# Two projection blocks in turn over each group of x, and first loads issued one behind another

## The chip, the cores and the metric

One core of one Trainium2 chip runs the whole program. The metric is the device time of one execution in microseconds (us), as the median of several runs. One further execution is recorded by the hardware profiler, and all rows below come from it.

## The reference, cut to what matters

The reference is a chain of transformer-like layers over 256 rows of x with 2048 columns, all in float32. Only its very first step matters here:

```
def layer_even(x, norm_g, w_in, w_out):
    h = rmsnorm(x, norm_g)                      # x * rsqrt(mean(x^2) + eps) * g
    qa, ka, ... , gate = split_cols(h @ w_in, SPLIT0)
```

`x` is 256x2048 (2 MB), `w_in` is 2048x6992. The product `h @ w_in` needs x turned (columns on the partitions) and every row scaled by its root mean square. The kernel multiplies the turned x by the gain first, forms the product, and scales the rows when the result leaves PSUM, so that the product can start before the sum of squares is known.

## The kernel before, in words

**Units and blocks.** All weights are read once, in units of 4 x 128 rows by 512 columns (1 MB). Four units (all 2048 rows) make one block of 512 result columns. Unit u of the whole program lands in slot u modulo 4 of `raw`. `plan` (L88) lays blocks one after another; `in_turn` (L98) can interleave the units of several blocks. The first ten blocks, L0_QKV, are w_in0's first columns. A block's result stands in a pair of PSUM banks, and the pairs alternate from block to block.

**Each product in three.** A float32 product is made of three cheaper ones: every weight is split in `w_hi` (ScalarE, `split_hi`, L1379) and `w_lo` = raw - w_hi (VectorE, `split_lo`, L2022), every x in `x_hi` and `x_lo`. TensorE adds w_hi x_hi, w_lo x_hi and w_hi x_lo (L685, L686, L688 or L694). One unit is 4 chunks x 2 row tiles x 3 = 24 matmuls.

**Preparing x.** x goes in four groups of 512 columns (`res`). For a group TensorE turns eight 128x128 tiles into PSUM banks 6 and 7 (`turn_group`, L784, matmuls of L781). VectorE multiplies by the gain (`gained`, L2133, two instructions). ScalarE makes `x_hi` of each (L1562), VectorE `x_lo` (L2140). The first matmul of a unit that uses a new group waits for both tiles of x_hi (`st_hi`, in `staged`, L790); the part with x_lo comes last in such a unit, behind a wait for `st_done`.

**The order.** Before, unit g of block 0 needs x group g, so four units in a row each need a new half MB of x. `first_block` turns group 1 behind the first chunk of unit 0, and group g+1 ahead of unit g after that. Units 0 and 1 are split in quarters (`first_hi`, L1385, and `first_lo`, L2028), so that a product can start when a quarter is ready. All engines run their instructions in the written order. ScalarE and VectorE split unit u+2 while unit u is multiplied (`advance`, L1494 and L2082; PARTS = 2).

**The loads.** SyncE issues all loads of x and weights. `load_block` (L508) issues x's first tile (L514), its second (L515), unit 0 in four quarters (L520), and then in turn x group 1 (L517), unit 1 (L503), group 2, unit 2, group 3, unit 3, with no wait between them. From unit 4 on a load waits until TensorE has used the unit that was in its slot (`parts_used`, L502). ScalarE issues the identity matrix and the gain columns (L1365, L1366) at the start.

**Leaving PSUM.** When a block is complete, ScalarE copies its two banks out, scaled by `rstd` (`drain`, L1403, L1416). rstd needs the squares of all four groups of x (`res_norm`, L1531, L1458). The block after next, which takes the same banks, waits for that copy.

The diff touches the plan of the first blocks (L119), the loads (L508 to L540, L575), and `first_block` on TensorE (L795, called at L1049), ScalarE (L1568, called at L1760) and VectorE (L2143, called at L2520).

Of the kernel before, what the change touches and what calls it, by code (L numbers as in the profile page):

```python
# [14 lines left out]
P = 128  # L15
SEQ = 256
NT = SEQ // P
D = 2048
KC = D // P
BW = 512  # L20
UC = 4
UNIT = UC * BW
RAW = 4
# [59 lines left out]
def build(nc, t):  # L83
# [4 lines left out]
    def plan(w, c0, widths, chunks=KC):  # L88
        first = len(blocks)
        for width in widths:  # L90
            in_turn([(w, c0, width, [(k, min(UC, chunks - k)) for k in range(0, chunks, UC)])])
            c0 += width
        return first
# [22 lines left out]
        plan(w, 2 * BW, [BW] * 2)  # L116
        return first

    L0_QKV = plan(t["w_in0"], 0, [BW] * 9 + [G0 - 9 * BW])  # L119
    L0_GATE = plan(t["w_in0"], G0, [BW] * 4)  # L120
    L0_OUT = out_blocks(t["w_out0"])
    L1_QKV = plan(t["w_in1"], 0, [BW] * 6)
# [54 lines left out]
    with ExitStack() as ctx:  # L177
# [251 lines left out]
        def first_part_landed(k):  # L429
            return first_parts_landed[k] if k < UC - 1 else raw_landed[0]  # L430
# [67 lines left out]
        def _(sp):  # L498
            def load(u, j, dst, src, first=False):

                if not first:
                    sp.wait_ge(parts_used, u - (RAW - 1))  # L502
                sp.dma_start(dst, src).then_inc(raw_landed[j], 16)  # L503

            def slot(j, chunks, width):
                return raw[:, j, :].rearrange("p (k n) -> p k n", k=UC)[:, 0:chunks, 0:width]

            def load_block(b):  # L508
                u, w, c0, width, units = blocks[b]
                for g, (k0, n) in enumerate(units):  # L510
                    if b == L0_QKV:
                        c = slice(g * BW, (g + 1) * BW)
                        if g == 0:
                            sp.dma_start(res[:, 0, c], t["x"][:, 0, c]).then_inc(x_first_tile_landed, 16)  # L514
                            sp.dma_start(res[:, 1, c], t["x"][:, 1, c]).then_inc(x_landed[0], 16)  # L515
                        else:
                            sp.dma_start(res[:, :, c], t["x"][:, :, c]).then_inc(x_landed[g], 16)  # L517
                        if g == 0:
                            for k in range(UC):
                                sp.dma_start(slot(0, UC, width)[:, k], w[k * P:(k + 1) * P, c0:c0 + width]).then_inc(  # L520
                                    first_part_landed(k), 16)
                            continue
                    j = (u + g) % RAW
                    load(u + g, j, slot(j, n, width),
                         w[k0 * P:(k0 + n) * P, c0:c0 + width].rearrange("(k p) n -> p k n", p=P), u < RAW)

            def load_units(u0, u1):
                for u in range(u0, u1):
                    b, place = block_of[u]
                    _, w, c0, width, units = blocks[b]  # L530
                    j = u % RAW
                    if b in CMP:
                        w1 = t[("cmp_k_w1", "cmp_v_w1")[CMP.index(b)]]
                        load(u, j, raw[:, j, :].rearrange("p (l n) -> p l n", l=8),
                             w1[place * 1024:(place + 1) * 1024, :].rearrange("(l p) n -> p l n", p=P))
                    else:
                        k0, n = units[place]
                        load(u, j, slot(j, n, width),
                             w[k0 * P:(k0 + n) * P, c0:c0 + width].rearrange("(k p) n -> p k n", p=P))

            def load_run(b, count):
                u, w, c0, width, units = blocks[b]

                def body(n, i, r):
                    for j, (k0, m) in enumerate(units):
                        load(n * 4 + (u + j), j, slot(j, m, width),
                             w[k0 * P:(k0 + m) * P, bass.ds(n * BW + c0, BW)].rearrange("(k p) n -> p k n", p=P))

                each(sp, count, body)
# [22 lines left out]
            def load_gain(row):  # L572
                sp.dma_start(grow, t["rows"][row:row + 1, :].to_broadcast([P, D])).then_inc(grow_landed, 16)

            load_block(L0_QKV)  # L575
            load_run(L0_QKV + 1, 8)
            load_block(L0_QKV + 9)
            for b in range(4):
                load_block(L0_GATE + b)
# [87 lines left out]
        def _(pe):  # L667
            at = [0]
# [115 lines left out]
            def turn_group(name, g, src, ready):  # L784

                for tt in range(NT):
                    ready(2 * g + tt)
                    turn(name, 2 * g + tt, [src(tt, g * UC + c) for c in range(UC)], gain=True)

            def staged(name, g, next_unit):  # L790

                pe.wait_ge(st_hi, turned_before[name] + 2 * g + 2)
                next_unit(g, lambda: pe.wait_ge(st_done, turned_before[name] + 2 * g + 2))

            def first_block(name, src, ready, next_unit):  # L795

                turn_group(name, 0, src, ready)
                if name == "n0":
                    products_of_ones(4)
                staged(name, 0, lambda g, low: next_unit(g, low, lambda: turn_group(name, 1, src, ready)))  # L800
                for g in range(1, 4):
                    if g < 3:
                        turn_group(name, g + 1, src, ready)
                    staged(name, g, next_unit)

            def tiled_first_block(name, src, ready, next_unit, others=()):

# [233 lines left out]
            def products_of_ones(n):  # L1041

                for _ in range(n):
                    nc.tensor.matmul(ps[:, 5, 0:P], ones[:], ones[:], start=True, stop=True)
# [1 line left out]
            pe.wait_ge(made["const_made"], 1)  # L1046
            products_of_ones(10)
            pe.wait_ge(ident_landed, 16)
            first_block("n0", of_res, lambda s: pe.wait_ge(x_landed[s // 2] if s else x_first_tile_landed, 16),  # L1049
                        next_in_plan)  # L1050
            advance(20)
            advance(3)

            def turn_idx(p):
# [309 lines left out]
        def _(act):  # L1364
# [34 lines left out]
            def split_next(u):  # L1399
                if u < N_UNITS:  # L1400
                    split_hi(u, u % RAW)
# [163 lines left out]
                        nc.scalar.activation(dst, ps[:, 6 + s % 2, :].rearrange("p (k n) -> p k n", k=UC),  # L1565
                                             ACT.Copy).then_inc(st_hi, 1)

            def first_block(name, gain=True, norm=None, held=False):  # L1568
                if held:
                    split_next(at[0] + 1)  # L1570
                if name == "n0":
                    first_hi(0, 1)
                hi_group(name, 0, gain)
                if name == "n0":
                    first_hi(1, UC)
                    first_hi(0, 2, 1)
                for g in range(4):
                    if g < 3:
                        hi_group(name, g + 1, gain)
                    if name == "n0" and g == 0:  # L1580
                        first_hi(2, UC, 1)
                    if norm:
                        norm(g)
                    advance(1)

            def tiled_first_block(name, norm, others=()):
# [170 lines left out]
                    act.wait_ge(x_first_tile_landed, 16)  # L1757
                act.wait_ge(x_landed[g], 16)

            first_block("n0", norm=res_norm(x_there))  # L1760
            advance(20)
            advance(3)

            def copy_idx(p):
# [244 lines left out]
        def _(dve):  # L2009
# [68 lines left out]
            def split_next(u):  # L2078
                if u < N_UNITS:
                    split_lo(u, u % RAW)  # L2080
# [59 lines left out]
                    V.tensor_tensor(x_lo[c], gained[:, tt] if gain else banks[tt], x_hi[c].bitcast(F32),  # L2140
                                    ALU.subtract).then_inc(st_done, 1)

            def first_block(name, gain=True, norm=None, held=False, update=None):  # L2143

                def ahead(g):
                    return (lambda: update(g)) if update and g < 4 else None

                if update:
                    update(0)
                lo_group(name, 0, gain, (lambda: first_lo(0, UC)) if name == "n0" else ahead(1))  # L2150
                if held:
                    split_next(at[0] + 1)
                def parts_of(g):

                    return (lambda: first_lo(0, UC, 1)) if g == 1 else (lambda: split_next(g))

                for g in range(4):
                    if g < 3:
                        lo_group(name, g + 1, gain, parts_of(g + 1) if name == "n0" else ahead(g + 2))
                    elif norm:  # L2160
                        norm()
                    advance(1, held=name == "n0" and g < 2)

            def gain_tile(name, g, tt):

# [351 lines left out]


            dve.wait_ge(cols_landed, 16)
            first_block("n0", norm=reciprocal_root)  # L2520
            advance(20)
            dve.wait_ge(const_landed, ALL_CONST)
            dve.wait_ge(made["const_made"], 1)
            all_drained(dve, L0_QKV + 6)
# [462 lines left out]
```

## Time and profile before

| what | value |
|---|---|
| median of 3 runs | 2884.12 us (2883.91 to 2885.12) |
| span of the profiled execution | 2882.2 us |
| profiled execution's own time | its span; what lies around it is not recorded (the median is 1.9 us above the span) |
| TensorE busy | 2865.5 us, 99% |
| weight loads into TensorE | 2396.2 us, 83% |
| VectorE busy | 1725.7 us, 60% |
| ScalarE busy | 1298.2 us, 45% |
| bytes moved | 530.60 MB, mean 184 GB/s |

Busy time is the time in which at least one instruction of the engine is under way. The span runs from the first to the last instruction. In timelines a bracket behind a row gives the idle time of that engine just before it and what ended it.

### The profile page before, as it was taken

What the parts mean: (1) busy time and instruction counts of PE and PEld (TensorE: products, weight loads), DVE (VectorE), ACT (ScalarE), POOL (GpSimd) and SP (SyncE); (2) the same over time, 40 slices, a digit from 0 to 9 for tenths busy, and PEclk for the clock granted to TensorE, in tenths of its full rate; (3) what the DMA queues carried; (4) which work ended last, traced back from release to release, by engine and by line L of the source; (5) the groups of instructions that cost most, each with busy time, mean ns of one, the idle gap of its engine ahead of it and who ended that gap; (6) DMA issues with size and microseconds to landing.
All of it is one profiled execution on the core that took longest, in us unless ns stands there. A gap on an engine that the chain in (4) does not pass through costs nothing.

```text
span 2882.2 us, 33404 instructions
## 1 busy us (share of the span) xinstructions
PE 2865.5 (99%) x13584; PEld 2396.2 (83%) x13584; DVE 1725.7 (60%) x1643; ACT 1298.2 (45%) x1350; POOL 14.4 (1%) x20
## 2 busy tenths in 40 slices
PE   9999999999999999999999999999999999999998
PEld 8878888888898888888888888888888888888887
DVE  5469856455565655555555677676755555555575
ACT  5344545354544533333333455545533334333354
POOL 0000000000000000000000000000000000000000
PEclk9999999999999999999999999999999999999999
DMA  7545355555445655555555557543655555555554
GB/s 249 191 157 189 116 191 179 197 178 167 156 151 198 197 191 192 192 190 193 191 190 189 190 173 245 174 150 120 224 190 189 190 190 188 190 190 192 192 180 155
DMA packets 275999, 530.60 MB, mean 184 GB/s; under 512 B 8768, under 2 KB 32464, under 8 KB 275392
## 3 DMA queue, kind: packets, MB, share of 16 engines
q1 hardware_dynamic: 274864, 527.01, 55.7%
q0 software_dynamic: 752, 2.04, 0.2%
q8 instruction: 70, 1.15, 0.2%
q10 hardware_dynamic: 288, 0.20, 0.0%
q14 instruction: 25, 0.20, 0.0%
HBM read 527.12 MB, written 2.10 MB: 184 GB/s over the span
## 4 chain that ended last, share of the span: by engine, by line
PE 96%; DVE 2%; ACT 1%; issue 1%; DMA 0%; SPq 0%; DVEq 0%; ACTq 0%
PE ps L685 29%; PE ps L686 29%; PE ps L688 27%; PE ps L694 2%; PE ps L882 1%; PE ps L781 1%; PE ps L713 1%; PE ps L714 1%; PE ps L718 1%; DVE w_lo L2025 1%; ACT w_hi L1383 1%; PE ps L869 1%; PE ps L902 1%; PE ps L913 0%; PE ps L914 0%
## 5 line engine op out<-in xcount | busy, mean ns | idle before, releaser
L2025 DVE TENSOR_TENSOR w_lo<-raw,w_hi 128x2048 fp32r<-128x2048 f32 (+3 forms) x505 | 1125.1, 2231 | 731.5 <-ACT w_hi L1383 730.6
L1383 ACT ACTIVATE w_hi<-raw 128x2048 fp32r<-128x2048 f32 (+3 forms) x505 | 941.8, 1868 | 990.3 <-DMA raw<-in_ff_w_down 318.0
L685 PE MATMUL ps<-w_hi,x_hi 128*128 128x512 f32 (+4 forms) x3168 | 1229.0, 388 | 2.5 <-DVE w_lo L2025 1.4
L686 PE MATMUL ps<-w_lo,x_hi 128*128 128x512 f32 (+4 forms) x3168 | 1217.3, 384 | 0.0
L688 PE MATMUL ps<-w_hi,x_lo 128*128 128x512 f32 (+3 forms) x2944 | 1130.8, 384 | 0.0
L685 PEld LDWEIGHTS ps<-w_hi,x_hi 128*128 128x128 f32 x3168 | 595.0, 188 | 120.6 <-issue 4.8
L686 PEld LDWEIGHTS ps<-w_lo,x_hi 128*128 128x128 f32 x3168 | 595.3, 188 | 112.7
L688 PEld LDWEIGHTS ps<-w_hi,x_lo 128*128 128x128 f32 x2944 | 552.7, 188 | 108.5
L685 PE MATMUL ps<-w_hi,h_hi 128*128 128x512 f32 x640 | 249.1, 389 | 0.0
L688 PE MATMUL ps<-w_hi,h_lo 128*128 128x512 f32 x640 | 249.0, 389 | 0.0
L686 PE MATMUL ps<-w_lo,h_hi 128*128 128x512 f32 x640 | 249.0, 389 | 0.0
L2679 DVE TENSOR_TENSOR z<-z,ps 128x1024 f32<-128x1024 f32 x86 | 105.0, 1221 | 111.6 <-PE ps L688 111.5
L688 PEld LDWEIGHTS ps<-w_hi,h_lo 128*128 128x128 f32 x640 | 120.1, 188 | 24.9
L686 PEld LDWEIGHTS ps<-w_lo,h_hi 128*128 128x128 f32 x640 | 120.1, 188 | 24.9
L685 PEld LDWEIGHTS ps<-w_hi,h_hi 128*128 128x128 f32 x640 | 120.1, 188 | 24.8
L1638 ACT ACTIVATE work<-ps 128x512 f32<-128x512 f32 (+1 forms) x48 | 25.1, 523 | 100.8 <-PE ps L869 97.2
L1416 ACT ACTIVATE z<-ps,st 128x512 f32<-128x512 f32 (+3 forms) x56 | 34.3, 664 | 65.6 <-PE ps L688 62.3
L1836 ACT ACTIVATE h_hi<-ps 128x512 fp32r<-128x512 f32 x40 | 21.8, 596 | 83.2 <-PE ps L781 83.2
L694 PE MATMUL ps<-w_hi,x_lo 128*128 128x512 f32 x224 | 55.4, 389 | 0.0
L2659 DVE TENSOR_TENSOR h_lo<-ps,h_hi 128x512 fp32r<-128x512 f32 x40 | 25.8, 686 | 49.3 <-ACT h_hi L1836 49.3
L1645 ACT ACTIVATE work<-work,st 128x128 f32<-128x128 f32 x80 | 35.8, 448 | 41.4 <-DVE st L2275 41.4
L1458 ACT ACTIVATE scaled<-res 128x512 f32<-128x512 f32 x56 | 34.7, 621 | 43.5 <-DVE res L2046 33.0
(333 smaller groups left out, 1597.0 us busy)
## 6 DMA issues: line engine op xcount, KB each, us to landing
raw<-in_w_in SPq DMA_DIRECT2D x139, 1024.0 KB, 5.0
raw<-in_ff_w_gate SPq DMA_DIRECT2D x88, 1024.0 KB, 5.2
raw<-in_ff_w_up SPq DMA_DIRECT2D x88, 1024.0 KB, 5.2
raw<-in_ff_w_down SPq DMA_DIRECT2D x88, 1024.0 KB, 5.1
raw<-in_w_out SPq DMA_DIRECT2D x45, 1024.0 KB, 5.1
raw<-in_w_ple_gate SPq DMA_DIRECT2D x16, 1024.0 KB, 5.1
raw<-in_w_in SPq DMA_DIRECT2D x8, 696.0 KB, 4.2
raw<-in_w_in SPq DMA_DIRECT2D x8, 520.0 KB, 3.7
```

The lines of the kernel that those rows point to most:

```text
L685: nc.tensor.matmul(o, x[0][:, k0 + c, s], hi[:, c, 0:width], start=first and c == 0, stop=False)
L686: nc.tensor.matmul(o, x[0][:, k0 + c, s], lo[:, c, 0:width], start=False, stop=False)
L688: m = nc.tensor.matmul(o, x[1][:, k0 + c, s], hi[:, c, 0:width], start=False, stop=last and c == n - 1)
L694: m = nc.tensor.matmul(ps[:, bank + tt, 0:width], x[1][:, k0 + c, tt * P:(tt + 1) * P], hi[:, c, 0:width], start=False, stop=last and c == ...
L713: nc.tensor.matmul(o, x[0][:, k0 + c, s], hi[:, c, 0:width], start=first and c == 0, stop=False)
L714: nc.tensor.matmul(o, x[0][:, k0 + c, s], lo[:, c, 0:width], start=False, stop=False)
L1383: nc.scalar.activation(landed_part(w_hi, u, j), landed_part(raw, u, j), ACT.Copy).then_inc(hi_ready, 1)
L1416: i = nc.scalar.activation(place_of(b)[:, tt], summed(b)[:, tt], ACT.Copy, scale=rstd[:, tt:tt + 1])
L1458: i = nc.scalar.activation(scaled[:, tt, 0:BW], rows[tt], ACT.Square, accum_out=sums[:, tt, j:j + 1])
L1645: i = nc.scalar.activation(prob[:, n % 2, keys_of[tt]], neg[:, n % 2, keys_of[tt]], ACT.Exp, scale=-1.0, bias=low[:, n % 2, tt:tt + 1], ac ...
L2025: V.tensor_tensor(landed_part(w_lo, u, j), landed_part(raw, u, j), landed_part(w_hi, u, j).bitcast(F32), ALU.subtract).then_inc(parts_read ...
L2679: V.tensor_tensor(o, o, ps[:, bank:bank + 2, :], ALU.add).then_inc(added, 1)
```

## The change

The units of blocks 0 and 1 are now numbered in turn: unit 0 is block 0's rows of group 0, unit 1 is block 1's rows of group 0, unit 2 is block 0's of group 1, and so on to unit 7. Each group of x serves two units in a row. TensorE turns group g+1 between the two units that use group g. On ScalarE and VectorE the work on group g+1 stands between the split of unit 2g+2 and that of unit 2g+3. Unit 0 is multiplied with its x_lo part last, as are units 2, 4 and 6; nothing is turned inside unit 0 any more.

SyncE issues three loads at once (x tile 0, quarter 0 of unit 0, x tile 1) and then each further one only behind a wait for the landing of an earlier one.

```
-    L0_QKV = plan(t["w_in0"], 0, [BW] * 9 + [G0 - 9 * BW])
+    all_chunks = [(k, UC) for k in range(0, KC, UC)]
+    L0_QKV = in_turn([(t["w_in0"], 0, BW, all_chunks), (t["w_in0"], BW, BW, all_chunks)], [0, 1] * 4)
+    plan(t["w_in0"], 2 * BW, [BW] * 7 + [G0 - 9 * BW])
...
+                rows_of_x(0, x_first_tile_landed, slice(0, 1))
+                first_weights(0)
+                rows_of_x(0, x_landed[0], slice(1, 2))
+                sp.wait_ge(x_first_tile_landed, 16)
+                first_weights(1)
+                sp.wait_ge(first_part_landed(0), 16)
+                first_weights(2)
+                sp.wait_ge(x_landed[0], 16)
+                first_weights(3)
+                sp.wait_ge(first_part_landed(1), 16)
+                load_units(1, 2, True)
+                sp.wait_ge(first_part_landed(3), 16)
+                rows_of_x(1, x_landed[1])
+                sp.wait_ge(raw_landed[1], 16)
+                load_units(2, 3, True)
+                sp.wait_ge(x_landed[1], 16)
+                load_units(3, 4, True)
+                sp.wait_ge(raw_landed[2], 16)
+                rows_of_x(2, x_landed[2])
+                load_units(4, 5)
+                rows_of_x(3, x_landed[3])
+                load_units(5, end_unit[L0_QKV + 1])
...
+            def first_blocks(name, src, ready):            (TensorE)
                 turn_group(name, 0, src, ready)
+                products_of_ones(4)
+                for g in range(4):
+                    staged(name, g, next_in_plan)
                     if g < 3:
                         turn_group(name, g + 1, src, ready)
-                    staged(name, g, next_unit)
+                    advance(1)
...
+            def first_blocks(name, norm):                  (ScalarE)
+                first_hi(0, 1)
+                hi_group(name, 0)
+                first_hi(1, UC)
+                first_hi(0, UC, 1)
                 for g in range(4):
+                    norm(g)
+                    advance(1)
                     if g < 3:
+                        hi_group(name, g + 1)
                     advance(1)
...
+            def first_blocks(name, norm):                  (VectorE)
+                lo_group(name, 0, between=lambda: first_lo(0, UC))
+                first_lo(0, UC, 1)
                 for g in range(4):
+                    if g == 3:
+                        norm()
+                    advance(1)
                     if g < 3:
+                        lo_group(name, g + 1)
+                    advance(1)
```

`rows_of_x(g, landed, tiles)` loads group g of x, `first_weights(k)` quarter k of unit 0, `load_units(a, b, True)` units a to b-1 without the wait for the slot. Behind the eight units each engine goes on with `advance(16)` where `advance(20)` stood.

## Rows read from the trace of the kernel before

**Rows 1.** The page: busy time by engine, then the chain that ended last.
```profile
PE 2865.5 (99%) x13584; PEld 2396.2 (83%) x13584; DVE 1725.7 (60%) x1643; ACT 1298.2 (45%) x1350; POOL 14.4 (1%) x20
...
PE 96%; DVE 2%; ACT 1%; issue 1%; DMA 0%; SPq 0%; DVEq 0%; ACTq 0%
```

**Rows 2.** Waits of TensorE up to 60 us: total, times, longest.
```profile
PE ps L781 <- DMA res<-in_x: 1.2, 2, 0.7
PE ps L1044 <- POOL ones L642: 1.0, 1, 1.0
PE ps L685 <- ACT x_hi L1562: 0.9, 1, 0.9
```

**Rows 3.** Timeline of TensorE: start, us, engine, line, operation, tiles.
```profile
6.95 0.66 PE L781 MATMUL ps<-ident,res 128*128 128x128 f32 x4 [0.65 <-DMA res<-in_x]
...
9.41 0.50 PE L685 MATMUL ps<-w_hi,x_hi 128*128 128x512 f32 x1 [0.90 <-ACT x_hi L1562]
...
17.49 0.48 PE L685 MATMUL ps<-w_hi,x_hi 128*128 128x512 f32 x1
...
23.03 1.04 PE L781 MATMUL ps<-ident,res 128*128 128x128 f32 x8
...
23.82 0.47 PE L685 MATMUL ps<-w_hi,x_hi 128*128 128x512 f32 x1
...
29.39 0.39 PE L685 MATMUL ps<-w_hi,x_hi 128*128 128x512 f32 x1
...
34.83 0.39 PE L685 MATMUL ps<-w_hi,x_hi 128*128 128x512 f32 x1
```

**Rows 4.** DMA totals of 0 to 4.5 us, then of 9 to 20 us.
```profile
DMA packets 434, 0.57 MB, mean 126 GB/s; under 512 B 34, under 2 KB 215, under 8 KB 434
...
DMA packets 2177, 4.29 MB, mean 390 GB/s; under 512 B 83, under 2 KB 83, under 8 KB 2177
```

**Rows 5.** Timeline of SyncE's issues (SPq), VectorE and ScalarE, columns as rows 3.
```profile
0.75 0.39 SPq L514 DMA_DIRECT2D res<-in_x  x1
...
5.67 1.15 SPq L503 DMA_DIRECT2D raw<-in_w_in  x1
...
7.11 1.29 DVE L2133 TENSOR_TENSOR gained<-ps,cols 128x512 f32<-128x512 f32 x2 [7.11 <-DMA cols<-in_cols]
...
17.00 0.62 ACT L1458 ACTIVATE scaled<-res 128x512 f32<-128x512 f32 x1
...
18.35 1.92 ACT L1383 ACTIVATE w_hi<-raw 128x2048 fp32r<-128x2048 f32 x1
...
20.30 2.29 DVE L2025 TENSOR_TENSOR w_lo<-raw,w_hi 128x2048 fp32r<-128x2048 f32 x1
...
22.51 1.29 DVE L2140 TENSOR_TENSOR x_lo<-gained,x_hi 128x512 fp32r<-128x512 f32 x2
```

**Rows 6.** Issue to landing: L514, L520, 1024 KB, 520 KB, L503 of 30-180 us.
```profile
DMA to landing us min/median/max: 4.1/4.1/4.1
...
DMA to landing us min/median/max: 6.0/6.3/6.6
...
raw<-in_w_in SPq DMA_DIRECT2D x139, 1024.0 KB, 5.0
...
raw<-in_w_in SPq DMA_DIRECT2D x8, 520.0 KB, 3.7
...
DMA to landing us min/median/max: 4.8/5.0/6.3
```

**Rows 7.** One x_hi instruction (L1562), and the copy out of PSUM (L1416, page).
```profile
L1562 ACT ACTIVATE x_hi<-gained x8: 614/618/633, 8.2 to 25.0; 128x512 fp32r<-128x512 f32 x8
...
L1416 ACT ACTIVATE z<-ps,st 128x512 f32<-128x512 f32 (+3 forms) x56 | 34.3, 664 | 65.6 <-PE ps L688 62.3
```

**Rows 8.** Products of ones on TensorE at the start, same columns as rows 3.
```profile
1.00 4.63 PE L1044 MATMUL ps<-ones 128*128 128x128 f32 x20 [1.00 <-POOL ones L642]
...
7.45 1.06 PE L1044 MATMUL ps<-ones 128*128 128x128 f32 x8
```

**Rows 9.** Stretches at the end: from:to, sum, busy of engines, granted clock, DMA.
```profile
2874.00:2876.00 2.00, 0.01 (x1) 0.00 (x0) 1.93 (x4) 1.96 (x4) 0.00 (x0) 1.00 0.53 218
2876.00:2877.00 1.00, 0.00 (x0) 0.00 (x0) 0.96 (x3) 0.11 (x1) 0.00 (x0) 0.79 0.88 350
2877.00:2879.00 2.00, 0.00 (x0) 0.00 (x0) 2.00 (x4) 0.00 (x0) 0.00 (x0) 0.50 0.88 316
```

**Rows 10.** The longest wait of TensorE in the whole execution, columns as in rows 2.
```profile
PE ps L713 <- ACT x_hi L1548: 1.7, 1, 1.7
```

More of the change, by code:

```diff
@@ L506, in slot @@
                 return raw[:, j, :].rearrange("p (k n) -> p k n", k=UC)[:, 0:chunks, 0:width]
-            def load_block(b):
[L509 to L525, printed above, removed]
@@ L527, in load_units, with load_first, rows_of_x, first_weights @@
-            def load_units(u0, u1):
+            def load_first():
+                def rows_of_x(g, landed, tiles=slice(0, NT)):
+                    c = slice(g * BW, (g + 1) * BW)
+                    sp.dma_start(res[:, tiles, c], t["x"][:, tiles, c]).then_inc(landed, 16)
+                def first_weights(k):
+                    sp.dma_start(slot(0, UC, BW)[:, k], t["w_in0"][k * P:(k + 1) * P, 0:BW]).then_inc(
+                        first_part_landed(k), 16)
+                rows_of_x(0, x_first_tile_landed, slice(0, 1))
[20 more added lines that the diff above has]
+                load_units(5, end_unit[L0_QKV + 1])
@@ L528, in load_units @@
+            def load_block(b):
+                load_units(first_unit[b], end_unit[b])
+            def load_units(u0, u1, first=False):
                 for u in range(u0, u1):
@@ L538, in load_units @@
                         load(u, j, slot(j, n, width),
-                             w[k0 * P:(k0 + n) * P, c0:c0 + width].rearrange("(k p) n -> p k n", p=P))
+                             w[k0 * P:(k0 + n) * P, c0:c0 + width].rearrange("(k p) n -> p k n", p=P), first)
             def load_run(b, count):
@@ L573, in load_gain @@
                 sp.dma_start(grow, t["rows"][row:row + 1, :].to_broadcast([P, D])).then_inc(grow_landed, 16)
-            load_block(L0_QKV)
-            load_run(L0_QKV + 1, 8)
+            load_first()
+            load_run(L0_QKV + 2, 7)
             load_block(L0_QKV + 9)
@@ L793, in staged, with first_blocks @@
                 next_unit(g, lambda: pe.wait_ge(st_done, turned_before[name] + 2 * g + 2))
-            def first_block(name, src, ready, next_unit):
+            def first_blocks(name, src, ready):
                 turn_group(name, 0, src, ready)
[L798 to L801, printed above, removed]
+                products_of_ones(4)
+                for g in range(4):
+                    staged(name, g, next_in_plan)
                     if g < 3:
                         turn_group(name, g + 1, src, ready)
-                    staged(name, g, next_unit)
+                    advance(1)
             def tiled_first_block(name, src, ready, next_unit, others=()):
@@ L1048, in _ @@
             pe.wait_ge(ident_landed, 16)
-            first_block("n0", of_res, lambda s: pe.wait_ge(x_landed[s // 2] if s else x_first_tile_landed, 16),
-                        next_in_plan)
-            advance(20)
+            first_blocks("n0", of_res, lambda s: pe.wait_ge(x_landed[s // 2] if s else x_first_tile_landed, 16))
+            advance(16)
             advance(3)
@@ L1566, in hi_group, with first_blocks @@
                                              ACT.Copy).then_inc(st_hi, 1)
[L1568 to L1576, printed above, removed]
+            def first_blocks(name, norm):
+                first_hi(0, 1)
+                hi_group(name, 0)
+                first_hi(1, UC)
+                first_hi(0, UC, 1)
                 for g in range(4):
+                    norm(g)
+                    advance(1)
                     if g < 3:
[L1579 to L1583, printed above, removed]
+                        hi_group(name, g + 1)
                     advance(1)
@@ L1758, in x_there @@
                 act.wait_ge(x_landed[g], 16)
-            first_block("n0", norm=res_norm(x_there))
-            advance(20)
+            first_blocks("n0", res_norm(x_there))
+            advance(16)
             advance(3)
@@ L2141, in lo_group, with first_blocks @@
                                     ALU.subtract).then_inc(st_done, 1)
[L2143 to L2155, printed above, removed]
+            def first_blocks(name, norm):
+                lo_group(name, 0, between=lambda: first_lo(0, UC))
+                first_lo(0, UC, 1)
                 for g in range(4):
+                    if g == 3:
+                        norm()
+                    advance(1)
                     if g < 3:
[L2159 to L2162, printed above, removed]
+                        lo_group(name, g + 1)
+                    advance(1)
             def gain_tile(name, g, tt):
@@ L2519, in _ @@
             dve.wait_ge(cols_landed, 16)
-            first_block("n0", norm=reciprocal_root)
-            advance(20)
+            first_blocks("n0", reciprocal_root)
+            advance(16)
             dve.wait_ge(const_landed, ALL_CONST)
```

## The prediction, made before the change was run

> **What bounds the kernel now.** I read the page first: the reader sees TensorE busy in 99% of the span, and the chain that ended last lies on it for 96% [rows 1]. So the time is TensorE's work plus its few gaps, and an edit to the first 50 us can only move its gaps there. The waits of TensorE are read next, up to 60 us: three rows that sum to 3.1 us [rows 2]. The timeline says when its work starts. Its first real matmul is at 9.41 us, unit 1 begins at 17.49, unit 2 at 23.82, unit 3 at 29.39, unit 4 at 34.83 [rows 3]. A unit is thus 5.44 us (34.83 - 29.39), and turning a group of x 0.79 us (23.82 - 23.03). Between 9.41 and 17.49 lie 5.44 + 0.79 us of work and 1.85 us that are the wait for group 1 of x (the second part of the 1.2 us in [rows 2]), slower first matmuls and issue. So at most 1.85 us can be had behind 9.41, and ahead of it what an earlier landing gives.
>
> The last view is the DMAs. Without waits in front, they come through at 390 GB/s from 9 to 20 us, but in the first 4.5 us only 0.57 MB move [rows 4].
>
> **The change part by part.** The work of TensorE stays: the same matmuls, turns and products of ones. Only the moments change, so I follow the one chain that decides.
>
> *Where the two kernels can be compared.* Before, when unit 2 begins at 23.82, all four groups are turned. After, when unit 2 begins, groups 2 and 3 are still to be turned: 2 x 0.79 = 1.58 us. Everything behind is the same. So unit 2 of the new kernel must begin at 23.82 - 1.58 = 22.24 us for no change; each us later is one us lost.
>
> *The start.* The chain to the first matmul is: x tile 1 lands and is turned (6.95 before), `gained` twice from 7.11, x_hi, 9.41 [rows 3, 5]. Quarter 0 of unit 0 moves ahead of x tile 1, and nothing else is in SyncE's queue. If the few loads land sooner, at best about 5.6 us, the start moves to 8.0; if the first packets are slow whatever stands behind them, it stays at 9.4, or is 0.7 later (256 KB at 390 GB/s [rows 4]). I take 9.0. This doesn't set the end, as follows.
>
> *The new waits of SyncE.* Queued behind each wait is every later load. The chain to unit 2's landing is: x tile 0 (L514, issued at 0.75 [rows 5], first in the queue now as then) lands 4.1 us later [rows 6], at 4.85; quarter 1 is issued at 4.9; when it lands, unit 1 is issued; when that lands, unit 2. Before, unit 2 was issued at 5.67, with nothing waited for [rows 5]. The price of a load with little in front of it: 520 KB take 3.7 us and 1024 KB 5.0 [rows 6], so 504 KB cost 1.3 us, and 256 KB would take 3.0; the quarters of unit 0 took 6.0 to 6.6 behind a full queue. I take 3.1, the nearest rows being those without a full queue. For 1 MB I take 5.0 (4.8 to 6.3 between 30 and 180 us [rows 6], where one load at a time is in flight). Then quarter 1 lands at 8.0, unit 1 at 13.05, unit 2 at 18.1, with 0.05 for each issue.
>
> The Trainium skill ("DMA: Bandwidth & Descriptors", Anatomy of one DMA) gives a DMA a fixed 2.0 us plus its bytes at 436 GB/s. By it 1 MB would be 4.4 us, an estimate that disagrees with the 5.0 of the rows, and the loss below would be 1.2 us smaller. That page speaks of GpSimd's path; the sum goes by the rows.
>
> *From landing to the first matmul.* VectorE's order is now: split of unit 2, then `gained` of group 1. So TensorE, which waits for x_hi of group 1 before unit 2, waits for: w_hi 1.92, w_lo 2.21 (20.30 to 22.51), `gained` 1.29, x_hi of its second tile 0.62, issue 0.05 [rows 5, 7]. Together 6.1 us. Unit 2 begins at 18.1 + 6.1 = 24.2 us.
>
> *Is TensorE busy until then?* x group 1 is issued when quarter 3 has landed (at the latest about 10.5) and its half MB follows unit 1's bytes: 13.05 + 1.35 = 14.4. Unit 0 from 9.0 ends at 14.5; group 1 is turned by 15.3; unit 1, by quarters, ends at 20.8 to 21.1. TensorE then idles about 3.2 us. The gap in front of unit 2 is late data, whether or not the start was earlier.
>
> *Behind unit 2.* x group 2 lands about 22, group 3 about 26, needed at 29.6 and later: hidden. `gained` of group 2 stands behind the split of unit 4 on VectorE: ScalarE is free at 24.2, w_hi of unit 3 to 26.1, squares of a group 1.35 (17.00 to 18.35 in [rows 5]), w_hi of unit 4 to 29.5, w_lo to 31.8, `gained` and x_hi to 33.7, and TensorE needs it at 24.2 + 5.44 + 0.79 + 5.44 = 35.9. It costs nothing, with 2 us of cover; without cover it costs 1:1. Block 2 needs block 0's banks, whose copy (2 x 0.66 us [rows 7]) now begins after unit 6 and lies beside unit 7's 5.44 us: nothing; uncovered it would be 1.3 us. The constants on GpSimd wait for group 3, 7 us later than now: nobody needs them early. I put these edits at 0.
>
> *Sum.* 24.2 - 22.24 = +2.0 us. Against the span of 2882.2 that is 2884.2; the median stands 1.9 us above the span, so I forecast 2886.1 us.
>
> **Bounds.** The chain at its shortest: quarter 1 in 3.0, both units in 4.8, x tile 0 one us earlier: 16.5, hence 22.6 and +0.4. At its longest: quarter 1 in 6.2 and one unit in 6.3: 4.9 + 6.2 + 0.05 + 5.0 + 0.05 + 6.3 = 22.5, hence 28.6 and +6.4.
>
> **The rivals.**
>
> *Forecast, slower by late data:* 2885.0 to 2887.5. Chance 0.45. For it speaks that three round trips stand in a row where 10.6 us of bytes were queued before.
>
> *The clock falls in the gap.* At the end of the kernel TensorE is busy for only 0.01 us behind 2874; the granted clock is 1.00 to 2876, 0.79 in the next us and 0.50 (1.2 GHz) after it [rows 9]. A mean of 0.79 puts the fall at 2876.6 ((1 - 0.79) / 0.5 = 0.42 us at the lower level), 2.6 us after the last matmul. At the start 20 passes of ones take 4.63 us (0.23 each), later 8 take 1.06 of which the last is drawn out: under 0.13 each [rows 8]. So it needs up to 5 us of work at half pace to come back, and loses half of that: 2.5 us on top. Time 2888.6. Chance 0.27: the gap of about 3.2 us is just longer than 2.6, and the longest wait of the kernel before is 1.7 us [rows 10], so there is none to compare. The Trainium skill ("TensorE: Matmul & The Clock Gate", Part 1) says that an idle array goes back to 1.2 GHz; by that rule this rival would be the likelier one, and the rows at the end agree with it.
>
> *Not slower: the short queue pays.* If unit 2 has landed and been split by the time TensorE is through, that is lands by 22.24 - 6.1 = 16.1 us, the gap is gone. With a start at 8.0, units 0 and 1 and one turn end at 8.0 + 5.44 + 0.79 + 5.44 = 19.7, with 0.6 of slower matmuls 20.3; gain 1.9, time 2882.2. For it speaks that half as much x is wanted per unit; against it that two loads of 1 MB take 10 us from issue to issue. Chance 0.18.
>
> *The first loads are slow on their own.* If the first 5 us are slow because of the packets themselves, quarter 1 takes 6.2 us as now and the longest chain above holds: 2890.5. Chance 0.10.
>
> **How the numbers follow.** The range of 8 in 10 goes from 2882.4 (leaving out about half of the third case) to 2889.4 (leaving out most of the last). Within 0.2%, which is 5.8 us and about what a measurement of this kernel tells from no change, lie all cases but most of the last: faster 0.02, same 0.90, slower 0.08. Faster by 5.8 us would take more than the whole head can give.
>
> **What would show it.** In the new trace: unit 1 and 2 land near 13 and 18 us; TensorE has one gap of about 3 us ahead of the first matmul of unit 2, ended by ScalarE's x_hi, and VectorE's `gained` of group 1 stands right behind the w_lo of unit 2; unit 2 begins near 24.2. Wrong if TensorE has no gap over 1 us behind its first matmul, if unit 2 lands before 16, or if matmuls behind the gap start every 0.45 us and not every 0.23 (then the second case). If the span differs by more than the position of unit 2 explains, something behind the first eight units moved, which I put at nothing.

## The result, and the profile after

The changed kernel takes 2890.74 us in the median of 12 runs; the kernel before takes 2884.11 in 12 runs. That is 6.6 us or 0.21% slower, ratio 1.0021 with a 95% interval of 1.0014 to 1.0029. (One of its 12, at 3213 us, had a mean clock of 0.841 over the whole kernel and is left out of the ratio.) The other times of the changed kernel spread from 2888.4 to 2892.1. The forecast was 2886.1 with a range up to 2889.4: the sign and the place were right, the size was not.

The waits of TensorE up to 60 us in the changed kernel, to be held against [rows 2]: total, times, longest.

```profile
PE ps L704 <- ACT x_hi L1579: 3.8, 2, 3.3
PE ps L800 <- DMA res<-in_x: 1.7, 2, 1.4
PE ps L1062 <- POOL ones L661: 1.0, 1, 1.0
```

One new wait of 3.3 us, for x_hi. The timeline of TensorE in the changed kernel shows where it stands, and what comes behind it (L704, L705 and L707 are the L685, L686 and L688 of before; compare [rows 3]):

```profile
8.66 0.47 PE L704 MATMUL ps<-w_hi,x_hi 128*128 128x512 f32 x1 [0.58 <-ACT x_hi L1579]
...
16.12 1.09 PE L800 MATMUL ps<-ident,res 128*128 128x128 f32 x8 [1.41 <-DMA res<-in_x]
...
16.96 0.48 PE L704 MATMUL ps<-w_hi,x_hi 128*128 128x512 f32 x1
...
22.29 0.39 PE L707 MATMUL ps<-w_hi,x_lo 128*128 128x512 f32 x1
25.95 0.58 PE L704 MATMUL ps<-w_hi,x_hi 128*128 128x512 f32 x1 [3.27 <-ACT x_hi L1579]
26.33 0.63 PE L705 MATMUL ps<-w_lo,x_hi 128*128 128x512 f32 x1
26.76 0.63 PE L704 MATMUL ps<-w_hi,x_hi 128*128 128x512 f32 x1
...
29.70 0.40 PE L705 MATMUL ps<-w_lo,x_hi 128*128 128x512 f32 x1
29.94 0.40 PE L704 MATMUL ps<-w_hi,x_hi 128*128 128x512 f32 x1
```

The first matmul comes at 8.66, 0.75 us earlier than before. But unit 2 begins at 25.95, where 22.24 would be no change: +3.71 us. Behind the gap the matmuls start 0.43 us apart (26.33, 26.76), and only from 29.7 on 0.23 again. The stretches of the changed kernel (columns as in [rows 9]) show the granted clock beside it, and a second place further on:

```profile
22.00:26.00 4.00, 0.73 (x5) 0.27 (x3) 3.90 (x5) 1.33 (x3) 0.00 (x0) 1.00 0.99 315
26.00:30.00 4.00, 4.00 (x11) 3.14 (x12) 2.90 (x3) 3.28 (x6) 0.00 (x0) 0.57 1.04 392
30.00:34.00 4.00, 4.00 (x24) 3.37 (x22) 2.43 (x3) 1.56 (x1) 2.89 (x6) 1.00 0.52 176
...
1668.00:1671.00 3.00, 1.38 (x8) 0.68 (x6) 2.41 (x6) 2.97 (x5) 0.00 (x0) 1.00 0.35 70
1671.00:1675.00 4.00, 3.61 (x11) 2.96 (x12) 2.90 (x5) 0.87 (x2) 0.00 (x0) 0.57 0.56 214
```

In the 4 us from 26.00 on the mean clock is 0.57, so TensorE is at the lower level, 1.2 GHz, in most of them. The gap itself still has 1.00: the fall comes at its end, when unit 2 has just begun. It is again so near 1672 us, behind the wait of 1.7 us ahead of the mixer that the kernel before has as well [rows 10]. There the matching matmul begins at 1665.90, and its profiled execution stayed at full clock. First the kernel before, then the changed one:

```profile
1640.00:1690.00 50.00, 47.73 (x222) 38.22 (x221) 42.25 (x50) 27.68 (x48) 0.00 (x0) 1.00 0.46 146
...
1640.00:1690.00 50.00, 47.99 (x220) 38.86 (x219) 40.23 (x47) 25.92 (x41) 0.00 (x0) 0.97 0.48 153
```

The span grew from 2882.2 to 2888.8, by 6.6. By comparing the two traces matmul by matmul, the shift is 5.4 us at unit 5, 5.5 from unit 6 up to 1670 us, and then becomes 6.6. So 3.7 us are late data, 1.7 the clock behind unit 2, 1.1 the clock at 1672, net of what other waits gave back.

Why unit 2 is late stands in the timeline of ScalarE and VectorE (compare [rows 5]) and of SyncE's issues:

```profile
14.83 2.19 ACT L1409 ACTIVATE w_hi<-raw 128x512 fp32r<-128x512 f32 x4 [4.56 <-DMA raw<-in_w_in]
...
19.79 1.92 ACT L1400 ACTIVATE w_hi<-raw 128x2048 fp32r<-128x2048 f32 x1 [1.54 <-DMA raw<-in_w_in]
24.67 1.23 ACT L1579 ACTIVATE x_hi<-gained 128x512 fp32r<-128x512 f32 x2 [2.96 <-DVE gained L2144]
```

```profile
21.74 2.29 DVE L2036 TENSOR_TENSOR w_lo<-raw,w_hi 128x2048 fp32r<-128x2048 f32 x1 [3.75 <-ACT w_hi L1400]
23.95 1.28 DVE L2144 TENSOR_TENSOR gained<-ps,cols 128x512 f32<-128x512 f32 x2
```

```profile
7.44 0.38 SPq L505 DMA_DIRECT2D raw<-in_w_in  x1
9.63 0.38 SPq L514 DMA_DIRECT2D res<-in_x  x1
14.82 1.63 SPq L505 DMA_DIRECT2D raw<-in_w_in  x2
```

Unit 1 is issued at 7.44 and lands at 14.8, unit 2 is issued at 14.82 and lands at 19.75, and from there the chain w_hi, w_lo, `gained`, x_hi takes 6.2 us, `gained` right behind w_lo although group 1 of x had been turned at 17.

### The profile page after: what moved, and what is told of

Same layout as the page of the kernel before. It is cut to its first block, busy times and chain, and to the rows that moved or that the text cites. A ratio compares the mean times of both kernels' runs of the same rounds, so it can differ in the third digit from the quotient of the medians.

```text
span 2888.8 us, 33378 instructions
## 1 busy us (share of the span) xinstructions
PE 2868.9 (99%) x13584; PEld 2398.0 (83%) x13584; DVE 1725.9 (60%) x1643; ACT 1299.0 (45%) x1350; POOL 14.4 (1%) x20
## 4 chain that ended last, share of the span: by engine, by line
PE 96%; DVE 1%; ACT 1%; issue 1%; DMA 1%; DVEq 0%; ACTq 0%
PE ps L704 29%; PE ps L705 29%; PE ps L707 27%; PE ps L713 2%; PE ps L900 1%; PE ps L800 1%; PE ps L732 1%; PE ps L733 1%; PE ps L737 1%; ACT w_hi L1400 1%; DVE w_lo L2036 1%; PE ps L887 1%; PE ps L920 1%; DMA raw<-in_w_in 1%; PE ps L931 0%
## 5 line engine op out<-in xcount | busy, mean ns | idle before, releaser
L704 PE MATMUL ps<-w_hi,x_hi 128*128 128x512 f32 (+4 forms) x3168 | 1230.1, 388 | 5.5 <-ACT x_hi L1579 3.8
L705 PE MATMUL ps<-w_lo,x_hi 128*128 128x512 f32 (+4 forms) x3168 | 1218.3, 385 | 0.0
L707 PE MATMUL ps<-w_hi,x_lo 128*128 128x512 f32 (+3 forms) x2944 | 1130.8, 384 | 0.0
L704 PEld LDWEIGHTS ps<-w_hi,x_hi 128*128 128x128 f32 x3168 | 595.5, 188 | 124.6 <-issue 4.8
L705 PEld LDWEIGHTS ps<-w_lo,x_hi 128*128 128x128 f32 x3168 | 595.8, 188 | 113.1
L707 PEld LDWEIGHTS ps<-w_hi,x_lo 128*128 128x128 f32 x2944 | 552.7, 188 | 108.3
L704 PE MATMUL ps<-w_hi,h_hi 128*128 128x512 f32 x640 | 249.1, 389 | 0.0
L707 PE MATMUL ps<-w_hi,h_lo 128*128 128x512 f32 x640 | 249.0, 389 | 0.0
L705 PE MATMUL ps<-w_lo,h_hi 128*128 128x512 f32 x640 | 249.0, 389 | 0.0
L707 PEld LDWEIGHTS ps<-w_hi,h_lo 128*128 128x128 f32 x640 | 120.1, 188 | 24.9
L705 PEld LDWEIGHTS ps<-w_lo,h_hi 128*128 128x128 f32 x640 | 120.1, 188 | 24.9
L704 PEld LDWEIGHTS ps<-w_hi,h_hi 128*128 128x128 f32 x640 | 120.1, 188 | 24.9
```

The lines of the kernel that those rows point to most:

```text
L704: nc.tensor.matmul(o, x[0][:, k0 + c, s], hi[:, c, 0:width], start=first and c == 0, stop=False)
L705: nc.tensor.matmul(o, x[0][:, k0 + c, s], lo[:, c, 0:width], start=False, stop=False)
L707: m = nc.tensor.matmul(o, x[1][:, k0 + c, s], hi[:, c, 0:width], start=False, stop=last and c == n - 1)
```

## The experiments

Theory: the row of waits brings unit 2 late; TensorE's idle gap follows, and with it the clock falls. The main rival: the new order of work makes the gap, above all `gained` behind the split of unit 2 on VectorE. A second: the clock has nothing to do with it.

The median of the unchanged kernel beside a to d was 2884.27, beside e to h 2884.94, beside i, k, l and m 2884.12, beside n, o and q 2884.11.

**a_order_only**: the new order of work, the loads without waits.

```
-                sp.wait_ge(x_first_tile_landed, 16)
                 first_weights(1)
-                sp.wait_ge(first_part_landed(0), 16)
                 first_weights(2)
...            (all eight waits of the first loads taken out; the expectations count seven)
```

> The changed kernel without the seven waits of SyncE; the order of loads and of the work stays. Theory (the row of waits makes unit 2 land late, and that opens the gap): unit 2 lands at 16.0 to 17.0 us and not at 19.75, its first matmul comes at 22.2 to 23.0 and not at 25.95, the gap ahead of it is under 1.5 us and the clock stays at 2.4 GHz: median 2884 to 2885.5. Rival (the gap comes from VectorE's order, the split of unit 2 ahead of the gain of group 1, whatever the loads do): the gap stays over 2.5 us and the median over 2888.

2885.14 us (2884.7 to 2886.5), ratio 1.0003 (0.9994 to 1.0012). In the trace unit 2 lands at 16.65 and begins at 22.83. TensorE has no gap there. So the median is 5.6 us lower without the waits. Of what is left, 0.6 us are the late start of unit 2 (22.83 for 22.24), and that comes from the beginning: x tile 1, now behind quarter 0 in a full queue, is late, TensorE waits 1.8 us for it, and the clock is low already here. TensorE's timeline and the stretches of this kernel:

```profile
7.87 1.11 PE L792 MATMUL ps<-ident,res 128*128 128x128 f32 x4 [1.77 <-DMA res<-in_x]
```

```profile
4.00:7.00 3.00, 1.50 (x12) 1.07 (x10) 0.30 (x1) 0.63 (x1) 0.00 (x0) 1.00 0.95 321
7.00:11.00 4.00, 3.13 (x14) 3.05 (x15) 1.75 (x4) 1.88 (x4) 0.00 (x0) 0.57 1.06 405
```

**b_waits_only**: the order of work of before, the new loads with their new order.

```
-            load_block(L0_QKV)
-            load_run(L0_QKV + 1, 8)
+            load_first()
+            load_run(L0_QKV + 2, 7)
```

> The kernel before, with the new chain of waited loads alone. Theory (the waits cost by themselves): group 1 of x lands near 16 us and not at 11.2, TensorE stands 4 to 5 us inside unit 0 where it waited 0.8, median 2887 to 2891, the upper half if the clock falls. Rival (the waits are harmless, the new order is what loses): within 1 us of before, 2883 to 2885.2.

2892.36 us (2891.1 to 2892.9), ratio 1.0027 (1.0017 to 1.0038): 1.4 us over the expected upper end, and worse than both edits together. The new loads are the loss; the interleaving softens them, since unit 0 no longer needs group 1 of x. The edit also puts group 1 of x behind unit 1 and not ahead of it, so it doesn't part the waits from the order of the loads; a_order_only does, for the interleaved kernel. The trace has the gap inside unit 0, 4.67 us, and a clock that stays low for longer:

```profile
14.90 1.97 PE L798 MATMUL ps<-ident,res 128*128 128x128 f32 x8 [4.67 <-DMA res<-in_x]
```

```profile
14.00:21.00 7.00, 6.10 (x19) 5.16 (x20) 4.77 (x8) 4.63 (x11) 0.00 (x0) 0.51 0.95 323
21.00:25.00 4.00, 3.87 (x22) 3.01 (x21) 1.11 (x3) 1.55 (x2) 0.00 (x0) 1.00 0.44 121
```

**c_gained_first**: all waits kept, `gained` of each group g+1 ahead of the split of unit 2g+2 on VectorE, and x_hi of group 1 ahead of the split of unit 2 on ScalarE.

```
+                    if g == 0:
+                        hi_group(name, 1)                     (ScalarE, ahead of the split of unit 2)
...
+                        lo_group(name, g + 1, between=lambda: split_next(at[0] + PARTS))     (VectorE)
```

> The changed kernel with its waits, but the gain and x_hi of group g+1 stand ahead of the split of unit 2g+2 on VectorE, and for group 1 on ScalarE too. Theory (the gap is landing 19.75 plus a chain of 6.2 us, of which 2.0 are gain and x_hi behind the split): unit 2 begins at 24.0 and not at 25.95, the gap is 1.3 us, too short for the clock to fall: median about 2890.7 - 2.0 - 1.6 = 2887.1. Rival (the data alone sets the moment, the order on VectorE does not matter): unchanged, 2890 to 2891.

2886.82 us (2885.5 to 2888.1), ratio 1.0008 (0.9999 to 1.0017), within 0.3 us of what was expected. Unit 2 begins at 24.30 and the clock does not fall there. Behind the wait ahead of the mixer it does fall in this profiled execution (the second row, a stretch):

```profile
24.30 0.47 PE L704 MATMUL ps<-w_hi,x_hi 128*128 128x512 f32 x1 [1.61 <-DVE w_lo L2038]
...
1668.00:1672.00 4.00, 3.90 (x13) 3.22 (x14) 3.49 (x6) 0.63 (x1) 0.00 (x0) 0.60 0.49 188
```

The order of the work is thus the second cause, not a rival: given late data it adds 1.7 us (25.95 - 24.30), and with that makes a gap of 3.3 us, behind which the clock fell, of one of 1.6, behind which it didn't.

**d_fill**: 14 products of ones behind unit 1 (28 matmuls in the timeline, two for each of its products).

```
                     advance(1)
+                    if g == 0:
+                        products_of_ones(14)
```

> The changed kernel with 14 products of ones on TensorE behind unit 1, some 2.8 us, which lie in the gap and delay nothing. Theory (the idle gap lets the clock fall, eight matmuls at 0.43 us cost 1.6 us): unit 2 begins at 25.95 as before, its matmuls all 0.23 us apart, median about 1.6 us below the changed kernel, near 2889.1. Rival (the slow matmuls behind the gap come from the late data or are chance): median as the changed kernel, 2890.7.

2887.85 us (2887.3 to 2888.9), ratio 1.0012 (1.0003 to 1.0021), 2.9 us below the changed kernel and not 1.6. TensorE's timeline:

```profile
22.68 3.29 PE L1064 MATMUL ps<-ones 128*128 128x128 f32 x28
26.17 0.50 PE L704 MATMUL ps<-w_hi,x_hi 128*128 128x512 f32 x1 [0.21 <-ACT x_hi L1581]
26.51 0.40 PE L705 MATMUL ps<-w_lo,x_hi 128*128 128x512 f32 x1
```

Unit 2 begins 0.2 us later, and its matmuls are at full pace at once. Work that computes nothing wins time. This profiled execution has no fall at 1672 either, so the median difference holds more than one fall.

**g_fill_late**: the kernel before, with 7 products in its wait ahead of the mixer.

```
+                        if name == "mix" and g == 0 and tt == 0:
+                            for _ in range(7):
+                                nc.tensor.matmul(ps[:, 2 * pair_of[block_of[at[0]][0]], 0:P], ones[:], ones[:], ...)
```

> The kernel before, with 7 products of ones (about 1.4 us) on TensorE in its longest wait, 1.7 us ahead of the mixer's first matmul near 1664 us. Theory (in some executions, not in others, the clock falls in that wait; it is why the times of the kernel before lie in two groups, near 2884.0 and 2885.1): the upper group is gone, all times within 0.6 us of 2884.0, median 0.2 us below before. Rival (the two groups have another cause): the times spread as before, over 1.3 us or more.

2883.77 us, ratio 0.9999 (0.9990 to 1.0008). 7 of 11 times lie at 2883.6 to 2883.9, but 4 still at 2884.7 to 2885.1. The expectation failed: this wait alone does not make the second group. Whether it has a share in it, this doesn't tell; beside it the unchanged kernel had 19 of 33 times above 2884.7.

**l_before_filled**: the same, with 3 products between x tiles 0 and 1 and 8 in the place of 4 ahead of unit 0.

```
+                    if name == "n0" and g == 0 and tt == 1:
+                        products_of_ones(3)
...
-                    products_of_ones(4)
+                    products_of_ones(8)
```

> The kernel before with products of ones in three waits: 3 between the two tiles of x group 0, 8 in the place of 4 ahead of the first matmul, 7 ahead of the mixer. Theory (the second group of times near 2885.1 comes from a fall of the clock in one of these waits, early or late): all times within 0.6 us of 2884. Rival (another cause): some 4 of 11 above 2884.6, as in g_fill_late.

2883.72 us, all 11 times within 2883.54 to 2883.94, ratio 0.9997 (0.9988 to 1.0006). Beside it the unchanged kernel had 13 of 33 times above 2884.7. So the upper group of the kernel before goes with the waits that are filled here. That a fall of the clock in some executions makes it is inferred: no profiled execution of the kernel before has one, but a_order_only has one at the start, and the changed kernel, c, i and n have one ahead of the mixer, four of the eleven profiled executions in which that wait is not filled. No run fills the waits of the start alone, so the shares of the two places stay open.

**o_all_filled**: the changed kernel with products in all these waits (3, 7, 6 behind unit 0, 15 behind unit 1, 7 ahead of the mixer).

> The changed kernel with products of ones in all of TensorE's longer waits: 3 between the tiles of group 0, 7 ahead of unit 0, 6 behind unit 0, 15 behind unit 1, 7 ahead of the mixer. Theory (of the 6.6 us that the change costs 3.7 are late data and the rest falls of the clock): median 2887.3 to 2887.9, spread under 1 us where the changed kernel has 3.7. Rival (only the fall ahead of unit 2 counts): as d_fill, 2887.85 with a spread of 1.6.

2887.91 us (2887.35 to 2888.58), ratio 1.0012 (1.0003 to 1.0021); the median is just beyond the upper edge of what was expected, and so is the spread, 1.2 us. d_fill had 2887.85, so the median doesn't tell the theory from its rival; the fills beyond the one ahead of unit 2 show only in the spread (1.7 us in d_fill). Against l_before_filled, the kernel before with its waits filled, what is left is 2887.91 - 2883.72 = 4.2 us; the other 2.4 us of the 6.6 went with the fills. The profiled executions of the two lie 3.7 us apart, neither with a fall, and unit 2 begins at 25.56 here, 3.3 us behind 22.24. By these figures the late data are 3.3 to 4.2 us.

**i_x1_later** and **n_unit1_alone** ask why unit 1 took 7.4 us to land.

```
i_x1_later:
                 sp.wait_ge(first_part_landed(3), 16)
+                sp.wait_ge(raw_landed[1], 16)
                 rows_of_x(1, x_landed[1])
-                sp.wait_ge(raw_landed[1], 16)
                 load_units(2, 3, True)
n_unit1_alone:
-                sp.wait_ge(first_part_landed(1), 16)
+                sp.wait_ge(first_part_landed(3), 16)
                 load_units(1, 2, True)
-                sp.wait_ge(first_part_landed(3), 16)
                 rows_of_x(1, x_landed[1])
```

> The changed kernel with group 1 of x issued only when unit 1 has landed, just ahead of unit 2. In the changed kernel unit 1 took 7.4 us from issue to landing where 5.0 were forecast. Theory (it shares the engines with group 1 of x, which is on the way at the same time): unit 1 lands near 12.7 and not at 14.8; group 1 of x lands 16 to 16.5, unit 2 about 19.2; median 0 to 1.5 us below the changed kernel. Rival (the first megabytes come slowly whatever is beside them): unit 1 lands at 14.5 or later, x group 1 at 18, and the median is 1 to 3 us above the changed kernel.

> The changed kernel with unit 1 issued only when quarter 3 has landed (near 9.7 us), group 1 of x right behind it. In i_x1_later unit 1 took 7.1 us from 7.7 with only quarters 2 and 3 under way, and behind 12 us a mean DMA share of 0.39. Theory A (the quarters in front of it and an uneven backlog on the engines make it late): issued with nothing under way it takes 5.0 to 5.5 us, landing near 15. Theory B (in the first 15 us loads are slow by themselves): again about 7, landing 16.5 to 17, and the median is 1 to 3 us over the changed kernel.

Moving group 1 of x away left unit 1 at 7.1 us (issued 7.68, landed 14.8): sharing with x is refuted. The median was 2890.87 (ratio 1.0021, 1.0012 to 1.0030), neither the gain of the theory nor the loss of its rival: TensorE now waits 4.3 us ahead of turning group 1, with a fall of the clock at the end of it, and unit 2 begins at 28.23. Issued 2.1 us later, with all quarters landed, unit 1 took 5.0 us and landed at 14.75, the same moment; median 2890.45 (ratio 1.0022, 1.0013 to 1.0031). Unit 1 of i_x1_later, then unit 1 and x of n_unit1_alone, each with its KB and the us from issue to landing:

```profile
raw<-in_w_in SPq DMA_DIRECT2D x1, 1024.0 KB, 7.1
```

```profile
raw<-in_w_in SPq DMA_DIRECT2D x1, 1024.0 KB, 5.0
res<-in_x SPq DMA_DIRECT2D x1, 512.0 KB, 5.9
```

So the load itself is not slow that early; with quarters still under way the 2.1 us of head start are lost. But loads under way aren't enough to explain it. In b_waits_only unit 1 is issued at 7.75 behind the same quarters and takes 5.8 us (landed at 13.5):

```profile
raw<-in_w_in SPq DMA_DIRECT2D x1, 1024.0 KB, 5.8
```

There unit 1 is the next 512 rows of the same columns; in the changed kernel it is the next 512 columns of the same rows. c_gained_first and d_fill, measured beside b with the changed kernel's loads, have 7.4. No run parts the place of the bytes from what is under way. The stretches of i_x1_later (last two columns: busy share of the DMA engines, GB/s) say that the engines do not end together: from 12 to 14.8, with only unit 1 under way, they are busy for 0.39 of the time at 151 GB/s. In n_unit1_alone, where unit 1 and x go out together, it is 1.04 at 405 in the same stretch. Why they don't, no run shows; that stays open.

```profile
12.00:14.80 2.80, 2.80 (x13) 2.07 (x11) 0.43 (x1) 0.00 (x0) 0.00 (x0) 1.00 0.39 151
```

```profile
12.00:14.80 2.80, 2.66 (x12) 1.88 (x10) 0.29 (x1) 0.04 (x1) 0.00 (x0) 1.00 1.04 405
```

**Towards a better version: e, f, h, k, m, q.** Each keeps the interleaved order and `gained` ahead of the split.

```
e_x_first            no waits; x tile 1 ahead of quarter 0; ScalarE as in c_gained_first
f_one_wait           only the first wait (quarter 1 behind x tile 0); ScalarE as in c_gained_first
h_one_wait_filled    f_one_wait + 7 products ahead of the mixer
k_split_then_gain    f_one_wait, but ScalarE's w_hi of unit 2 ahead of x_hi of group 1
m_best               k_split_then_gain + 3, 7 (for 4) and 7 products of ones
q_quarters           m_best + unit 2 split in quarters:
-                by_part = isinstance(u, int) and u < 2
+                by_part = isinstance(u, int) and u < 3
...
+                    if g == 0:
+                        first_hi(0, UC, 2)
...            (and first_lo of unit 2 on VectorE)
```

> The interleaved order of work, no waits in SyncE's first loads, both tiles of x group 0 ahead of the quarters as in the kernel before, and gain and x_hi ahead of the split of unit 2. Theory (start 9.4, no gap: units 0 and 1 with one turn end at 21.7, unit 2 is split by 16.65 + 4.1 = 20.8): unit 2 begins at 21.7 against 22.24 for equality, median 0.5 us below before, 2883.6. Rival (interleaving itself costs something behind unit 2): at or above before.

> As the changed kernel, with only the first of the seven waits (quarter 1 behind x tile 0), and with gain and x_hi ahead of the split of unit 2. Theory (the first wait gives the early start of 8.7, the later ones only delay unit 2): unit 2 begins near 21.0, median 1.2 us below before, about 2883.0. Rival (the start stays early only while all waits hold the queue short): first matmul at 9.4 to 10.5, median 2883.6 to 2885.

> The last one, with the 7 products of ones in the wait ahead of the mixer as well. Theory (two gains add): median 0.2 to 0.5 below it, about 2882.7, with no second group of times. Rival (the second group comes from elsewhere): as it.

> Only the first wait of SyncE; on VectorE the gain of group g+1 ahead of the split of unit 2g+2; on ScalarE the order of the changed kernel (w_hi of unit 2 ahead of x_hi of group 1). Theory (in f_one_wait w_hi of unit 2 began at 18.26 only, behind x_hi, with its data there; this takes it away): w_hi from 17, w_lo done by 21.0, unit 2 begins near 21.2, against 22.6 there: median 1.2 us below f_one_wait, about 2883.3. Rival (data of unit 2 lands after 18 here, and the order doesn't matter): 2884 to 2885.

> k_split_then_gain with products of ones in the same three waits (7 in the place of 4 ahead of the first matmul). Theory: median 0 to 0.5 us below k_split_then_gain, 2882.8 to 2883.3, below the kernel before. Rival (the added products delay the first matmul, or the order brings nothing): 2884 or more.

> m_best with unit 2 split in quarters, as units 0 and 1. Theory (in k_split_then_gain and m_best TensorE still waits 0.4 to 0.56 us for the whole w_lo of unit 2): the wait goes, median 0.4 us below m_best, 2883.3, and below both kernels. Rival (ScalarE's and VectorE's longer quarters push x_hi of group 1 out by as much): as m_best, 2883.7 or more.

| kernel | median us | lowest to highest | ratio, 95% interval | unit 2 begins |
|---|---|---|---|---|
| e_x_first | 2884.28 | 2884.1 to 2885.4 | 1.0000 (0.9991 to 1.0009) | 22.43 |
| f_one_wait | 2884.70 | 2884.1 to 2885.6 | 1.0000 (0.9991 to 1.0009) | 22.63 |
| h_one_wait_filled | 2884.72 | 2884.2 to 2886.0 | 1.0000 (0.9991 to 1.0009) | 23.33 |
| k_split_then_gain | 2884.79 | 2883.3 to 2886.3 | 0.9999 (0.9990 to 1.0008) | 22.02 |
| m_best | 2883.72 | 2883.3 to 2884.1 | 0.9997 (0.9988 to 1.0006) | 22.28 |
| q_quarters | 2883.22 | 2882.8 to 2883.4 | 0.9996 (0.9987 to 1.0005) | 21.83 |

e missed by 0.7 us and f by 1.7 (beside them the unchanged kernel had 2884.94, so the miss against it is smaller; the ratio says no difference): with the data early, ScalarE's x_hi (waiting for `gained`) stood ahead of w_hi of unit 2 and held it. In f its w_hi began at 18.26, in e at 18.06. k took that away (17.63), but its times spread over 3.0 us, and its median missed too. h brought nothing; that its start isn't covered by the fill ahead of the mixer is the likely reason, not shown. m has k's lower end without the spread, 0.4 us over what was expected, and no better than l_before_filled. q met its expectation. Its last waits ahead of unit 2 are gone, all its 11 times lie below the lowest of the 27 unchanged runs beside it (2883.57). It beats both kernels by that; the interval of the ratio still takes in 1. Of its 0.9 us some 0.4 are the fills (2884.11 - 2883.72, by l_before_filled) and 0.5 the order (unit 2 at 21.83 for 22.24).

## Why the prediction missed its range, step by step

- *The place, and the measure at unit 2.* Right. One gap ahead of unit 2, ended by x_hi, `gained` right behind w_lo, and 22.24 us as the moment of no change: 25.95 gives +3.7, with all behind it hidden as forecast.
- *Landing to first matmul, 6.1 us.* Right: 6.2.
- *The start.* 8.66 for 9.0, and without effect on the end, as argued.
- *Quarter 1, 3.1 us.* Right side: it took 2.6 (issued at 4.84, landed at 7.4).
- *"For 1 MB I take 5.0".* This is the first step that failed, for unit 1: 7.4 us. The rows behind it were of a load with nothing under way; here two quarters were. n_unit1_alone shows that 5.0 holds once they have landed; with them under way it was 7.4 here and 5.8 in b_waits_only, so what makes it 7.4 stays open. Unit 2 took 4.9, as taken. The chain made 18.1; it was 19.75, and that is the 1.7 us between +2.0 and +3.7. The bound used for it, one unit at 6.3 us, was too low. (The shortest chain of the bounds adds up to 16.6, not 16.5; nothing hangs on it.)
- *"The clock falls in the gap", chance 0.27, and at nothing in the sum.* This is the second step that failed. It happened, and d_fill shows that it is caused by the idle gap. The gap of 3.2 us was longer than the 2.6 us of [rows 9] and still was made the less likely case. That one row is no measure either: the clock fell 1.2 us behind the last matmul in a_order_only, 3.5 us behind it in the changed kernel, and 5.1 us behind it at the end of q_quarters. In all four profiled executions with a gap of more than 3 us among the first units (the changed kernel, b, i, n) it fell. The sentence from the Trainium skill ("TensorE: Matmul & The Clock Gate", Part 1) was on the right side. The price was 1.7 us here, not 2.5: the lower clock lasted for eight matmuls.
- *What was not seen.* The clock can fall with waits of 1 to 2 us too, and the fall near 1672 us, 1.1 us net, lies where the prediction put everything at nothing. The three terms make the miss: 2886.1 + 1.7 + 1.7 + 1.1 = 2890.6, for 2890.7 measured. The prediction took the one profiled execution of before, without a fall, for the kernel, though the three known times (2883.9, 2884.1, 2885.1) already lay in two groups. Late data and the one fall behind unit 2 are +5.4 us, which is 2889.5 and just above the range already.
- *"Not slower: the short queue pays", chance 0.18.* Refuted in both halves: the earlier start of 0.75 us was real and was worth nothing behind late data.

## What to carry to other kernels

A wait for a landing turns a queue into a row of round trips. Here each 1 MB load cost 5 to 7 us that way, where its bytes are 2.7 us at the 390 GB/s of [rows 4], and the second consumer of each group of x did not make up for it; hold back only the loads that would delay the very first operands. Where an engine gets work that needs two inputs, put the part whose input comes first in front, and check the order again when the loads are changed: the best order for late data (c) was the wrong one for early data (f). And before judging a microsecond or two, look whether the times lie in groups, and whether a fall of TensorE's clock can separate them; products of ones in the known waits narrowed the times of both kernels, from 1.5 us and more to 0.4, and from 3.7 to 1.2.

## What the runs showed of the hardware

A wait of TensorE can cost half of its length or more once again behind it: 1.7 us (eight matmuls at 0.43 us and not 0.23) behind a gap of 3.3 us, and 1.1 us net near 1672 us behind a wait of 1.7 us, the latter in some executions only. The granted clock was still 1.00 in the gap of 3.3 us and fell when the work had begun again. In b_waits_only a gap of 4.7 us left a mean granted clock of 0.51 for 7 us. A wait of 1.8 us at the very start did it as well (a_order_only, 0.57 from 7 to 11 us). And one load of 1 MB landed at 14.8 whether it was issued at 7.7 behind unfinished loads or at 9.7 us behind finished ones; in b_waits_only, where it read other rows, it landed at 13.5.
